# Two-layer hybrid decoder trunk: the order of the attention stages, with queries of the later quarters beside the first attentions

## What is computed

```python
def hybrid_layer(x, c, positions, g_mix, g_mlp, w_ada, b_ada, w_in, qn_swa, kn_swa,
                 qn_moba, kn_moba, sinks, w_o_swa, w_o_moba, w_out, w_up, w_down):
    mod = jax.nn.silu(c) @ w_ada + b_ada
    sh1, sc1, gt1, sh2, sc2, gt2 = jnp.split(mod, 6, axis=-1)
    h = adaln(rms_norm(x, g_mix), sh1, sc1)
    proj = h @ w_in
    q_a, k_a, v_a, q_b, k_b, v_b, gate_a, gate_b = jnp.split(proj, IN_OFFSETS, axis=-1)
    ...
    y_a = swa_attention(q_a, k_a, v_a, sinks) @ w_o_swa
    y_b = moba_attention(q_b, k_b, v_b) @ w_o_moba
    mixed = jax.nn.sigmoid(gate_a) * y_a + jax.nn.sigmoid(gate_b) * y_b
    x = x + gt1[:, None, :] * (mixed @ w_out)
    h = adaln(rms_norm(x, g_mlp), sh2, sc2)
    u = jnp.square(jax.nn.relu(h @ w_up))
    x = x + gt2[:, None, :] * (u @ w_down)
    return x
```

## Time and profile before

| what | value |
|---|---|
| median of 3 runs | 2147.47 us (2146.55 to 2198.24) |
| the profiled execution | 2147.77 us |
| its span, slowest core (core 7) | 2145.9 us (the others 2138.7 to 2145.3) |
| PE busy | 2009.5 us, 94% |
| DVE, ACT, POOL busy | 60%, 44%, 12% |
| granted TensorE clock, mean of core 7 | 0.974 |

### The profile page before, as it was taken

The page is one execution under the profiler, slowest core; times in us unless marked ns, Lnnn a source line. Parts: engine busy times, 40 slices in busy tenths (PEclk is TensorE's granted clock), DMA queues, the critical chain, the costliest instruction groups (busy, mean ns, idle before and its releaser), DMA issues.

```text
span 2145.9 us, 36361 instructions; the slowest of 8 cores (2138.7 to 2145.9 us)
## 1 busy us (share of the span) xinstructions
PE 2009.5 (94%) x13004; PEld 950.7 (44%) x13004; DVE 1291.5 (60%) x2409; ACT 949.0 (44%) x1437; POOL 265.6 (12%) x259
## 2 busy tenths in 40 slices
PE   1899799999899999999999988999998999999999
PEld 1454344444354444444445434444444544444444
DVE  3589756453266656566569895554524765556665
ACT  2777664657744111111148765456585431111111
POOL 1345300000012000001002460000001200000000
PEclk9999799999999999999999997999999999999999
DMA  9956701000388171707330463101015905040022
GB/s 194 214 75 89 103 2 40 22 20 9 63 136 110 23 106 21 99 10 99 98 119 1 70 85 54 41 1 40 2 41 70 177 1 78 2 66 14 1 79 79
DMA packets 114926, 136.80 MB, mean 64 GB/s; under 512 B 3776, under 2 KB 100160, under 8 KB 113216
## 3 DMA queue, kind: packets, MB, share of 16 engines
q0 software_dynamic: 101200, 85.11, 29.2%
q1 hardware_dynamic: 13552, 49.37, 6.6%
HBM read 200.69 MB, written 18.87 MB: 102 GB/s over the span
## 4 chain that ended last, share of the span: by engine, by line
PE 89%; ACT 4%; issue 3%; DMA 2%; DVE 2%; SPq 0%; ACTq 0%; DVEq 0%
PE PS L625 87%; ACT SB L653 3%; PE PS L635 2%; DMA SB<-x 2%; DVE SB L658 1%; DMA SB<-w_ada 1%; ACT SB L692 0%; DVE SB L684 0%; SPq L715 0%; ACT L653 0%; ACT SB L886 0%; DVE SB L898 0%; ACT SB L908 0%; DVE SB L694 0%; DVE SB L674 0%
## 5 line engine op out<-in xcount | busy, mean ns | idle before, releaser
L625 PE MATMUL PS<-SB 128*128 128x512 bf16 (+6 forms) x12220 | 1975.7, 326 | 92.4 <-ACT SB L653 33.7
L625 PEld LDWEIGHTS PS<-SB 128*128 128x128 bf16 (+1 forms) x12220 | 899.1, 98 | 1114.1 <-issue 307.3
L653 ACT ACTIVATE SB<-PS 128x512 bf16<-128x512 f32 (+4 forms) x870 | 618.6, 736 | 969.9 <-PE PS L625 915.6
L658 DVE TENSOR_TENSOR SB<-SB 128x512 f32<-128x512 f32 (+6 forms) x704 | 455.3, 652 | 176.2 <-ACT SB L653 129.8
L658 DVE TENSOR_TENSOR SB<-PS,SB 128x512 f32<-128x512 f32 (+5 forms) x657 | 360.9, 558 | 149.8 <-PE PS L625 133.3
L684 DVE SCALAR_TENSOR_TENSOR SB<-PS,SB 128x512 bf16<-128x512 f32 x360 | 252.6, 706 | 269.1 <-ACT SB L653 268.5
L658 POOL TENSOR_TENSOR SB<-SB 128x512 bf16<-128x512 f32 (+2 forms) x94 | 124.4, 1333 | 473.5 <-DVE SB L684 394.0
L684 DVE SCALAR_TENSOR_TENSOR SB<-SB,PS 128x512 f32<-128x512 f32 x128 | 87.8, 687 | 144.7 <-PE PS L625 112.0
L635 PE MATMUL PS<-SB 128*128 128x128 bf16 x784 | 89.8, 232 | 39.3 <-DVE SB L898 23.8
L715 POOL DMA_DIRECT2D SB<-w_ada x48 | 40.4, 850 | 639.6 <-PE PS L625 602.1
L635 PEld LDWEIGHTS PS<-SB 128*128 128x128 bf16 x784 | 61.3, 104 | 75.9 <-issue 55.1
(11 more groups left out here) (25 smaller groups left out, 189.0 us busy)
## 6 DMA issues: line engine op xcount, KB each, us to landing
SB<-w_ada POOLq DMA_DIRECT2D x48, 512.0 KB, 8.3
SB<-w_in POOLq DMA_DIRECT2D x16, 1024.0 KB, 17.0
SB<-w_up POOLq DMA_DIRECT2D x16, 1024.0 KB, 12.0
SB<-w_down POOLq DMA_DIRECT2D x16, 1024.0 KB, 18.7
SB<-x SPq DMA_DIRECT2D x16, 512.0 KB, 13.7
SB<-x SPq DMA_DIRECT2D x8, 1024.0 KB, 7.5
xsp<-SB SPq DMA_DIRECT2D x4, 2048.0 KB, 7.6
SB<-xsp SPq DMA_DIRECT2D x8, 1024.0 KB, 7.4
```

What stands on the lines that cost most here:

```text
L625: ins = e.matmul(o.ap, l_.ap, rr.ap, start=a, stop=b)
L653: S.add([('act', lambda e, o=out, i=in_: e.activation(out=o.ap, in_=i.ap, func=func, **kw), d)], r, out.keys, tab=TABS.get(func))
L658: return e.tensor_tensor(out=o.ap, in0=a.ap, in1=b.ap, op=op)
```

## The change

Only numbers that set `vt`, and TAB_SLACK. The windows of keys and values are 15 apart and 18 long (17 and 20 before). The query windows are 26 apart and 14 long: T + 72 to 86, 98 to 112, 124 to 138 and 150 to 164 (before, 18 apart: T + 68 to 86, to 104, to 122, to 140). The first attention's window runs from 138 to 184 (before to 160), the third's from 240 to 326 (before to 320). The gates and output of the first quarter still begin at 165, those of the second at 252 and end at 344 (before 240 and 320), the gates of the third run from 332 to 396 (before 320 to 376). `c_mix` takes the first 80% of its stretch (before 70%). The adaLN gate comes 8 later, the norms of the MLP 4 later at their start. TAB_SLACK is 12 instead of 4.

```diff
-TAB_SLACK = 4.0
+TAB_SLACK = 12.0
...
                 kv_stage(l, s, W1)
-                S.window(i0, T + s * 17.0, T + s * 17.0 + 20.0)
+                S.window(i0, T + 0.0 + s * 15.0, T + 0.0 + s * 15.0 + 18.0)
...
                 q_stage(l, s, W1)
-                S.window(i0, T + 68.0 + 18.0 * s, T + 86.0 + 18.0 * s)
+                S.window(i0, T + 72.0 + 26.0 * s, T + 86.0 + 26.0 * s)
                 if s == 2:
                     i0 = len(S.ops)
                     ada_gate(l, 2048, gt1, [sb(T0 + 8192 + i * 4096, (8, 256), BF16) for i in range(2)], True)
-                    S.window(i0, T + 100.0, T + 136.0)
+                    S.window(i0, T + 108.0, T + 144.0)
             pool_banks[0] = [(6,), (7,)]
             WC = load_c(l, T + 60.0)
-            at_t = [(138, 160), (160, 240), (240, 320), (320, 400)]
-            c_t = [(165, 240), (240, 320), (320, 400), (400, 428)]
+            at_t = [(138, 184), (160, 240), (240, 326), (320, 400)]
+            c_t = [(165, 240), (252, 344), (332, 412)]
...
                     t0, t1 = c_t[s - 1]
-                    c_window(c_mix, t0, t0 * 0.3 + t1 * 0.7, s - 1, WC, mixs[0])
+                    c_window(c_mix, t0, t0 * 0.20000000000000007 + t1 * 0.7999999999999999, s - 1, WC, mixs[0])
                     if s < 3:
-                        c_window(c_out, t0 * 0.3 + t1 * 0.7, t1, l, s - 1, WC, mixs[0], ytmp[0])
+                        c_window(c_out, t0 * 0.20000000000000007 + t1 * 0.7999999999999999, t1, l, s - 1, WC, mixs[0], ytmp[0])
...
                 norm(s, A2(l), modv(l)[:, 24:32], h2(s))
-                S.window(i0, T - 56.0 + 28.0 * s, T - 36.0 + 28.0 * s)
+                S.window(i0, T + -52.0 + 28.0 * s, T + -34.0 + 28.0 * s)
```

## The result

The changed kernel takes 2123.27 us (median of 4 runs, 2122.98 to 2125.42) against 2147.35 us before on the same chip: ratio 0.9891, 95% interval 0.9872 to 0.9911, 1.1% less. Forecast were 2118 us within 2097 to 2146. Some executions were slowed on a die or on two cores: the times of the experiments are medians of the others, the ratios are of means (in e1, e7 and e8 with one execution that had two slowed cores, so there the median is the better reading), and of e5 cores 4 to 7 are read. The size was right to 5 us; the two parts of which it was summed were not.

What follows compares the result with a forecast made beforehand. TensorE was busy 94% of the span, with everything to win in the attention half. From 2147.8 us, 21.9 for mixing and 15 for the last attention's cover came off and 7 of prices were added: 2117.9 us, range 2097 to 2146.

Steps and rivals of the forecast that it cites:

- Part A: Last quarter's queries mixed with attention 0, filling a stretch where no engine is busy: 21.9 us won over two layers.
- With 88%, 48.0 becomes 54.5: Layer 0, last queries to attention 0's end: 48.0 us of DVE work at 88% busy shortens 65.3 us by 10.8.
- the prediction's own signs: 64-row matmuls by about 225, score matmuls near 380 ns, clock-0.5 stretch gone or halved, attention 0 ending near 268.
- Up to 12.6 us go to the clock: Layer 0, last queries and attention 0: PE's 25.1 busy us at 1.2 GHz would take about half at 2.4 GHz.
- rival 3: Both parts at their bounds, DVE full, last attention's tail gone, no prices: 2090 us; shorter PE steps speak for it; chance 0.17.
- the bound of PE: Last queries and attention 0, layer 0: PE at full clock needs 49.5 - 12.6 = 37 us, below DVE's 48.0.
- Part B: Third quarter's gates and second quarter's output cover the last attention's end, filling PE's waits for Exp: 15 us won.
- The price of 1.5 us a layer for attention 2's lost cover: Attention 2 (353:460) loses 13.5 us of output cover, bringing ACT to 70%: 1.5 us a layer, bounds 0 and 6.
- The loads: w_o_moba and gate weights issue later behind delayed query items, with 13 us of cover: 2 us a layer, bounds 0 and 13.
- Rival 4: First quarter's `c_mix` starves as w_o_moba and gate weights land after attention 0's end: slower, 2165 us; chance 0.06.
- The rest, at nothing: Key and value windows, adaLN gate, MLP norms under a full PE (577:650) and TAB_SLACK: no gain or loss counted.
- Rival 1: Query tiles keep breaking the bank pairs attention 0's scores need, so mixing gives 0: 2136 us; chance 0.22.

Runs made afterwards that it cites:

- e1: Kernel before with only the query windows, adaLN gate and first attention's window of the changed kernel: 2141.2 us against 2147.2, ratio 0.9982.
- e7: Kernel before plus 60 unread 128x512 matmuls per layer at lowest priority, filling PE gaps during attention 0: 2145.2 us against 2146.6, ratio 1.0009.
- e8: Kernel before with the third quarter's gates reaching from 332 to 396 and the changed kernel's norm windows: 2141.1 us against 2146.6.
- e5: Changed kernel with the last quarter's query tiles kept off banks 0, 1, 4 and 5: on cores 4 to 7 the last step ends 9.2 us earlier.
- e6: Changed kernel with the last quarter's query window drawn out to attention 0's end, T + 150 to 184: 2127.8 us, ratio to before 0.9911.
- e4: Changed kernel with the MLP norms' windows of the kernel before: 2128.9 us, ratio to before 0.9923.
- e10: Same kernel as e5 run again, the changed kernel with the last quarter's query tiles off banks 0, 1, 4, 5: 2117.5 us, ratio to before 0.9859.
- e12: e10 with many windows moved on (attentions, last queries, gates, output, norms): executions of 2090.8 to 2093.5 us, ratio to before 0.9741.

## Why the prediction was right, and which of its steps weren't

**Part A (forecast 21.9 us, less 4 for loads): mis-sized, 8.1 us.** The step that failed is "With 88%, 48.0 becomes 54.5". 88% held during the mix (36.85 of 42.1 us). It was applied to the whole stretch, though, and attention 0 lasts longer than its cover: the last quarter's window ends at 164, the attention's at 184. The chain alone needs 18.5 us more, at 50% of DVE; at 88% its 9.28 us of VectorE work would take 10.5. These 8 us are what layer 0 falls short by. The cover's end was missing from the working, though the windows of the diff tell of it, and the earlier trace rows have DVE at 55% (13.45 of 24.5 us) where attention 0 runs without queries. Of the prediction's own signs the start came (222, "by about 225"); the others didn't: the score matmuls of 64x512 take 474 ns and not 380, the half-clock time in the stretch falls from 28 to 19 us, and attention 0 ends at 274 and not 268.

```profile
L625 PE MATMUL PS<-SB 64*128 64x512 bf16 x24 | 5.4, 474 | 1.2 <-ACT SB L653 1.2
```

**The clock.** "Up to 12.6 us go to the clock", worked out for layer 0, was no term of the sum, but it stood behind rival 3 and the bound of PE. By e7 it is near nothing here, as far as its fillers allow to tell: with 17 to 21 us less at half clock the stretch is as long as before. My reading is that TensorE at half clock, where it waits for ScalarE and VectorE anyway, costs only what its slower steps add to the chain.

**Part B (forecast 15 us, less 3): 16.9 us, mis-sized low.** The mechanism was right: 49 wide matmuls where 3 were, PE 29.3 of 32. Of 8.5 and 9.2 us idle in the median core some 4 remain a layer, as forecast (3.0 in the last 32 us, 1.4 and 0.8 behind them); on the slowest core the w_ada wait of layer 0 is the largest piece. The price of 1.5 us a layer for attention 2's lost cover didn't show: PE is busy 97.28 of 101 us there (349:450), against 104.11 of 107, so 3.7 us idle instead of 2.9: less than a microsecond. The balance of the median core, from the first output to the last, shows what else was mis-sized: idle time and what half clock costs PE's busy time go together from 18.5 to 11.2 us in layer 0 and from 19.9 to 10.6 in layer 1, and 1.7 us of that a layer is half clock ahead of the last 32 us, which the forecast didn't count.

```profile
349.00:450.00 101.00, 97.28 (x897) 43.41 (x897) 50.67 (x151) 62.59 (x79) 1.26 (x1) 1.00 0.06 22
```

**The loads (forecast -4 us): covered.** w_o_moba is issued at 243.08 instead of 234.49, 8.6 us later and within the 13 of cover; in the waits of PE from 213 to 275 there is no DMA. Rival 4 didn't come; e6 doesn't test it either, since its last items ended no later and w_o_moba went out only 1.3 us later.

```profile
243.08 0.81 POOL L715 DMA_DIRECT2D SB<-w_o_moba  x1 [5.11 <-PE PS L625]
```

**"The rest, at nothing".** Right for the keys' windows and for TAB_SLACK, which change no instruction. Wrong for the norms: with the other edits in place they carry some 6 us (e4). "PE is busy 73.00 of 73" described the old order; in the new one the wait for w_ada, 2.90 us before, takes 3.9 us on the slowest core, and with the norms of before 5.7. That wait makes only a part of the 6.

**Rival 1, the banks.** It was written as all or nothing. What came is between: attention 0 did start at 222, and yet taking the shared banks away wins 6 to 9 us (e5, e10), with DVE at 93% instead of 88% during the mix.

The errors, 10 us too much in A with its loads and 5 too little in B, partly cancelled. That 2118 and 2123 lie so close is in that measure luck.

**Open:** why the planner's order is worse in e6, whether cover up to the end of attention 0 would help by itself, and how the norms reach the next layer's mixing. A small change of priority re-deals order and banks, and a few microseconds of any of these runs may be that.

## What to carry to other kernels

When a stage bound by one engine is laid beside a chain, work out two stretches, not one: as long as both have work the busiest engine's rate holds, and then the longer of the two runs alone. Let the cover outlast the chain (e12 does, among other edits, and its PE is full there), and try separate sets of PSUM banks where one side needs pairs and the other single banks (e5, e10: 6 to 9 us). Where all order comes from greedy priorities, compare the instruction order before measuring: two of these edits changed nothing at all, and one thought idle carried a quarter of the gain.

## What the hardware showed that wasn't expected

Taking half-clock time away from TensorE gave nothing measurable while its matmuls stood in a chain through ScalarE and VectorE: in e7 28.3 and 28.5 us at half clock became 11.4 and 7.0, with 60 more matmuls a layer, at a ratio of 1.0009 (0.9974 to 1.0044). The Trainium skill (TensorE: Matmul & The Clock Gate, Terms) puts the penalty at about the throttled time times the share withheld; by that 17 and 21 us less at half clock should have given some 19 us, an estimate. The run shows no such amount. The filling matmuls take PE time themselves, and what is measured is the gain less their delay: of that the interval allows 6 us at most.
